# A gated projection by Strassen's scheme: seven block products for eight on one core of a Trainium2

## The chip, the cores and the metric

The kernel is one program on one NeuronCore of a Trainium2 chip. Its metric is the device time of one execution, in microseconds (us). Three runs took 3548.36, 3549.2 and 3543.41 us; the median is 3548.36.

## What is computed

Two transformer blocks of two layers each run one after the other on 512 tokens of width 1024, all in float32. The second block's feed-forward parts are gated, and there are two of them per layer (ffn1 and ffn2), around a mixer:

```python
D_MODEL, SEQ, DEPTH, D_FF = 1024, 512, 2, 2816

def swiglu(h, w_gu, w_down):
    gu = h @ w_gu                                   # (512, 1024) @ (1024, 2 * 2816)
    g, u = gu[..., :D_FF], gu[..., D_FF:]
    return (jax.nn.silu(g) * u) @ w_down

def second_block(x, ...):
    for l in range(DEPTH):
        x = x + 0.5 * swiglu(rmsnorm_2(x, ffn1_norm[l]), ffn1_w_gu[l], ffn1_w_down[l])
        x = x + hybrid_mixing(rmsnorm_2(x, mix_norm[l]), ...)
        x = x + 0.5 * swiglu(rmsnorm_2(x, ffn2_norm[l]), ffn2_w_gu[l], ffn2_w_down[l])
    return rmsnorm_2(x, final_norm)
```

## The kernel before, in words

Activations lie transposed: channel on the 128 partitions, token along the free axis, so x_lat is 8 tiles of 128 x 512. Every float32 product is made of three products in the fp32r format: each operand is split into a high part (a copy rounded to fp32r) and a low part (the operand less its high part), and TensorE adds low weight x high input, high weight x low input and high weight x high input (L803 to L805).

The program is a list of stages; each engine walks it with its own instruction queue, and semaphores order them. A linear stage goes by chunks, one chunk being 128 output channels. For chunk g the SP queue loads the weight into w_raw (two slots in turn, `load_chunk`), ScalarE makes the high part w_hi_sb (`split`, L1380), VectorE the low part w_lo_sb (`split`, L1769), and TensorE runs kt x 3 matmuls of 512 columns, kt being 8 for an input of 1024 channels and 11 for the input of a down projection. ScalarE starts the high part of chunk g once TensorE has finished chunk g - 2, which had the same slot.

The gated stages are of the kind `linear_glu`. There are two layers, two parts and two groups of FG = 11 tiles of 128 channels, so 8 such stages and 88 steps of i. A step is two chunks: the gate's into bank 0 and the up projection's into bank 1. VectorE multiplies the gate by rstd2, the inverse root of the mean square of the input (L2228), ScalarE takes silu (L1691), VectorE multiplies the up projection by rstd2 (L2231) and by silu (L2236), ScalarE makes the high part of the result (L1405) and VectorE its low part (L1835). These steps stand in a hardware loop (`Fori`). After each gated stage a `linear_r` stage multiplies the 11 middle tiles by the down projection and adds the result to x_lat (L2165).

The input of a gated stage is x scaled by the norm's gain, without rstd: in the final `linear_r` stage before it (`final=True`), each finished tile of x_lat is scaled by VectorE (L2182, `prep`), ScalarE makes its high and VectorE its low part, while GpSimd squares the tile and adds it to a running sum (`sum_squares`, L2322 to L2325). In the first group's stage TensorE turns the sum into the mean (`norm_sum`, L812), ScalarE takes the root and VectorE the reciprocal (L1774, `deferred_rstd`).

The lines that the rows below name beside these: L1801 is a multiply and add of VectorE for block 1's conditioning, L2257 finds the maximum of attention scores in PSUM, L2354 is GpSimd's scaling of attention weights, L1672 is a copy of a bank by ScalarE.

```python
for k in range(kt):
    nc.tensor.matmul(dst, wl, hi[:, k, 0:n], start=(k == 0), stop=False)
    nc.tensor.matmul(dst, wh, lo[:, k, 0:n], start=False, stop=False)
    mm = nc.tensor.matmul(dst, wh, hi[:, k, 0:n], start=False, stop=(k == kt - 1))
```

Of the kernel before, what the change touches and what calls it, by code (L numbers as in the profile page):

```python
# [101 lines left out]
def build_program(nc, a, out):  # L102
    from contextlib import ExitStack
    ctx = ExitStack()
    with ctx:
# [27 lines left out]
        m2h = place("m2h", [P, FG, T], F32R, mid0)  # L133
        m2l = place("m2l", [P, FG, T], F32R, mid0 + FG * T * 4)
# [8 lines left out]
        h2h = place("h2h", [P, KD, T], F32R, z0)  # L143
        h2l = place("h2l", [P, KD, T], F32R, z0 + KD * T * 4)
        w_raw = place("w_raw", [P, 2, WMAX])
        w_hi_sb = place("w_hi_sb", [P, 2, WMAX], F32R)
        w_lo_sb = place("w_lo_sb", [P, 2, WMAX], F32R)
# [39 lines left out]
        def x_square(n):  # L187
# [14 lines left out]
                 "fox_vt fox_vc fox_a fox_e fox_c c_hi c_lo c_rows sel_done o_zero r_const bd_zero pool_s pool_m pool_y pool_t pool_hi pool_lo "  # L202
                 "x_sq x_sum rows_zero rows_turned rows_copied silu_done x_turned x_copied y_ready y_turned y_copied y_scaled "
                 "dve_chain act_chain pool_chain").split()
        dma_names = ("w_loaded0 w_loaded1 mod_loaded0 mod_loaded1 mod_loaded2 mod_loaded3 fd_loaded0 fd_loaded1 fd_loaded2 "
                     "ctx_loaded konst_loaded rows_loaded "
                     "x_loaded rope_loaded ws_loaded rf_loaded mla_loaded bd_loaded stored").split()
# [3 lines left out]
        fd_loaded = [S[f"fd_loaded{i}"] for i in range(3)]  # L211

# [37 lines left out]

        Stage("setup", {})
        Stage("mod", {})
        for l in range(L):
# [31 lines left out]
            for g in range(FF1_GROUPS):  # L285
# [4 lines left out]
                Stage("linear_r", dict(r_taken=8, sumsq=1 * last, norm_t=8 * ends, h_hi=8 * ends, h_lo=8 * ends,  # L290
                                       sq_part=int(split_sq > 0), sq_last=split_sq), 8,
                      src="w_ff2", l=l, sets=more, gate=gate(1), group=g, final=last, kt=KD,
                      prep=(R_F1, hh_lat, hl_lat) if ends else None, block2=ends)
        lat = ("lat",)
        for l in range(L):
# [6 lines left out]
            for part in ("ffn1", "mix", "ffn2"):  # L302
                if part == "mix":
# [11 lines left out]
                    Stage("linear_r", dict(r_taken=8, sumsq=1, norm_t=8, h_hi=8, h_lo=8), 8, src="w_out_2", l=l, sets=lat,  # L315
                          gate=one, group=None, final=True, kt=KD, prep=(R_F2 + KD * l, h2h, h2l), block2=True)
                else:
                    for g in range(F2_GROUPS):
                        n1 = int(g == 0)
                        Stage("linear_glu", dict(gate_taken=FG, up_taken=FG, silu_ready=FG, t_ready=FG, mid_hi=FG, mid_lo=FG,  # L320
                                                 sum_ready=n1, root_ready=n1, rstd_ready=n1), 2 * FG, l=l, sets=lat,
# [20 lines left out]
        def next_kt(st):  # L342
            i = linear.index(st)
            return kt_of(linear[i + 1]) if i + 1 < len(linear) else None
# [185 lines left out]
        def late_square(st, s):  # L530

            return glu_up if st.block2 else sq_late[s]
# [1876 lines left out]
```

## Time and profile before

| | |
|---|---|
| median of three runs | 3548.36 us (3543.41 to 3549.2) |
| span of the profiled execution | 3545.8 us, 47285 instructions |
| TensorE (PE) busy | 3438.6 us, 97% |
| weight loads (PEld) busy | 2871.9 us, 81% |
| VectorE (DVE) busy | 1832.1 us, 52% |
| ScalarE (ACT) busy | 1226.1 us, 35% |
| GpSimd (POOL) busy | 362.9 us, 10% |
| mean of the DMA engines | 30% busy, 89 GB/s |

The page gives no time of the profiled execution beside its span; the span lies 2.6 us below the median of the runs. Busy time is the sum of durations, where overlapping ones count once. A matmul's duration is modelled and overlaps that of the next, so what it costs is read from the distance between starts.

### The profile page before, as it was taken

What the parts mean: (1) busy time and instruction counts of PE and PEld (TensorE: products, weight loads), DVE (VectorE), ACT (ScalarE), POOL (GpSimd) and SP (SyncE); (2) the same over time, 40 slices, a digit from 0 to 9 for tenths busy, and PEclk for the clock granted to TensorE, in tenths of its full rate; (3) what the DMA queues carried; (4) which work ended last, traced back from release to release, by engine and by line L of the source; (5) the groups of instructions that cost most, each with busy time, mean ns of one, the idle gap of its engine ahead of it and who ended that gap; (6) DMA issues with size and microseconds to landing.
All of it is one profiled execution on the core that took longest, in us unless ns stands there. A gap on an engine that the chain in (4) does not pass through costs nothing.

```text
span 3545.8 us, 47285 instructions
## 1 busy us (share of the span) xinstructions
PE 3438.6 (97%) x17172; PEld 2871.9 (81%) x17172; DVE 1832.1 (52%) x2781; ACT 1226.1 (35%) x1930; POOL 362.9 (10%) x403
## 2 busy tenths in 40 slices
PE   9989999999999999999999989999999999899999
PEld 5879888888878878888888677888888886778887
DVE  6755866554356444354345655434543455654343
ACT  4455222122146432233222364323232223643232
POOL 0012300000202200010001223000200011230001
PEclk9989999999999999999999999999999999999999
DMA  6300243334220123333333301333333333023332
GB/s 223 117 24 13 95 136 113 119 121 134 60 72 25 48 83 96 100 96 95 95 94 107 89 25 51 98 97 99 95 95 95 95 101 83 25 60 95 98 98 89
DMA packets 551252, 314.76 MB, mean 89 GB/s; under 512 B 31102, under 2 KB 524888, under 8 KB 551128
## 3 DMA queue, kind: packets, MB, share of 16 engines
q1 hardware_dynamic: 550608, 312.99, 29.7%
q8 instruction: 76, 1.25, 0.2%
q14 instruction: 48, 0.39, 0.0%
q10 hardware_dynamic: 520, 0.13, 0.0%
HBM read 310.98 MB, written 2.10 MB: 88 GB/s over the span
## 4 chain that ended last, share of the span: by engine, by line
PE 88%; DVE 5%; ACT 4%; issue 2%; POOL 1%; DMA 0%; SPq 0%; DVEq 0%; ACTq 0%; POOLq 0%
PE ps L803 26%; PE ps L805 25%; PE ps L804 25%; PE ps L1349 3%; PE ps L1325 1%; DVE nmax L2257 1%; PE ps L958 1%; DVE scr L1946 1%; PE ps L1291 1%; ACT scr L1720 1%; ACT z L1720 1%; PE ps L1292 1%; ACT w_hi_sb L1380 1%; DVE hl_ctx L1835 1%; DVE hl_lat L1934 0%
## 5 line engine op out<-in xcount | busy, mean ns | idle before, releaser
L1769 DVE TENSOR_TENSOR w_lo_sb<-w_raw,w_hi_sb 128x1024 fp32r<-128x1024 f32 (+1 forms) x460 | 588.6, 1280 | 1231.3 <-ACT w_hi_sb L1380 1228.9
L1380 ACT ACTIVATE w_hi_sb<-w_raw 128x1024 fp32r<-128x1024 f32 (+1 forms) x460 | 506.3, 1101 | 1375.6 <-PE ps L805 1347.4
L803 PE MATMUL ps<-hh_lat,w_lo_sb 128*128 128x512 f32 x1808 | 719.4, 398 | 6.3 <-DVE w_lo_sb L1769 1.9
L804 PE MATMUL ps<-hl_lat,w_hi_sb 128*128 128x512 f32 x1808 | 705.2, 390 | 0.0
L805 PE MATMUL ps<-hh_lat,w_hi_sb 128*128 128x512 f32 x1808 | 704.8, 390 | 0.0
L803 PEld LDWEIGHTS ps<-hh_lat,w_lo_sb 128*128 128x128 f32 x1808 | 340.5, 188 | 85.1 <-issue 6.8
L804 PEld LDWEIGHTS ps<-hl_lat,w_hi_sb 128*128 128x128 f32 x1808 | 340.6, 188 | 74.8 <-issue 6.3
L805 PEld LDWEIGHTS ps<-hh_lat,w_hi_sb 128*128 128x128 f32 x1808 | 340.1, 188 | 71.8
L803 PE MATMUL ps<-h2h,w_lo_sb 128*128 128x512 f32 x704 | 275.2, 391 | 1.9 <-DVE z L2228 1.5
L803 PE MATMUL ps<-m2h,w_lo_sb 128*128 128x512 f32 x704 | 273.9, 389 | 0.0
L804 PE MATMUL ps<-h2l,w_hi_sb 128*128 128x512 f32 x704 | 273.9, 389 | 0.0
L805 PE MATMUL ps<-h2h,w_hi_sb 128*128 128x512 f32 x704 | 273.9, 389 | 0.0
L805 PE MATMUL ps<-m2h,w_hi_sb 128*128 128x512 f32 x704 | 273.9, 389 | 0.0
L804 PE MATMUL ps<-m2l,w_hi_sb 128*128 128x512 f32 x704 | 273.9, 389 | 0.0
L803 PE MATMUL ps<-m1h_lat,w_lo_sb 128*128 128x512 f32 x512 | 200.4, 391 | 2.7 <-DVE x_ctx L2165 2.7
L804 PE MATMUL ps<-m1l_lat,w_hi_sb 128*128 128x512 f32 x512 | 199.5, 390 | 0.0
L805 PE MATMUL ps<-m1h_lat,w_hi_sb 128*128 128x512 f32 x512 | 199.3, 389 | 0.0
L2322 POOL TENSOR_TENSOR x_ctx<-x_lat 128x512 f32<-128x512 f32 x7 | 7.3, 1042 | 1578.1 <-DVE x_lat L2165 1578.1
L803 PEld LDWEIGHTS ps<-h2h,w_lo_sb 128*128 128x128 f32 x704 | 132.1, 188 | 31.1 <-DVE z L2228 2.3
L804 PEld LDWEIGHTS ps<-h2l,w_hi_sb 128*128 128x128 f32 x704 | 132.1, 188 | 27.8 <-issue 0.5
L805 PEld LDWEIGHTS ps<-h2h,w_hi_sb 128*128 128x128 f32 x704 | 132.1, 188 | 27.6
L2354 POOL TENSOR_SCALAR scr<-scr,rinv 128x768 f32<-128x768 f32 (+4 forms) x120 | 89.4, 746 | 635.4 <-DVE rinv L2268 634.9
(329 smaller groups left out, 5520.8 us busy)
## 6 DMA issues: line engine op xcount, KB each, us to landing
w_raw<-in_ffn_w_gu SPq DMA_DIRECT2D x176, 512.0 KB, 3.8
w_raw<-in_w_ff SPq DMA_DIRECT2D x128, 512.0 KB, 4.1
w_raw<-in_ffn_w_down SPq DMA_DIRECT2D x64, 704.0 KB, 4.5
z<-in_w_mod SPq DMA_DIRECT2D x64, 512.0 KB, 5.2
w_raw<-in_w_in SPq DMA_DIRECT2D x56, 512.0 KB, 3.9
w_raw<-in_w_out SPq DMA_DIRECT2D x32, 512.0 KB, 3.9
scr<-in_w_mod SPq DMA_DIRECT2D x16, 512.0 KB, 5.2
scr<-in_w_mod SPq DMA_DIRECT2D x2, 2048.0 KB, 14.6
```

Of the source, the lines that this page charges most:

```text
L803: nc.tensor.matmul(dst, wl, hi[:, k, 0:n], start=(k == 0), stop=False)
L804: nc.tensor.matmul(dst, wh, lo[:, k, 0:n], start=False, stop=False)
L805: mm = nc.tensor.matmul(dst, wh, hi[:, k, 0:n], start=False, stop=(k == kt - 1))
L958: mm = nc.tensor.matmul(bank(5 + n % 3)[0:2, :], silu_c[:, :, k], mod_slot(n)[:, k, :], start=(k == 0), stop=(k == KD - 1))
L1291: nc.tensor.matmul(dst[:, c0:c1], q, k_hi[:, hd // 4, c0:c1], start=True, stop=False)
L1292: mm = nc.tensor.matmul(dst[:, c0:c1], q, k_lo[hd // 4][:, c0:c1], start=False, stop=True)
L1325: mm = nc.tensor.transpose(bank(4 + i % 2)[:, j * P:(j + 1) * P], p[:, kt * P:(kt + 1) * P], ident)
L1349: mm = nc.tensor.matmul(bank(6 + hd % 2)[:, qt * P:(qt + 1) * P], val, att_pt(st, v, kt * P, (kt + 1) * P), start=(kt == 0), stop=(kt == n ...
L1380: nc.scalar.activation(w_hi_sb[:, slot, 0:width], w_raw[:, slot, 0:width], ACT.Copy).then_inc(S["w_hi"], 1)
L1720: nc.scalar.activation(att_p(st, u, n), s_slot(st, u, n), ACT.Exp, bias=nmax[:, i:i + 1], scale=q_scale(st, u) if st.first else 1.0, accum ...
L1769: nc.vector.tensor_tensor(w_lo_sb[:, slot, 0:width], w_raw[:, slot, 0:width], w_hi_sb[:, slot, 0:width].bitcast(F32), ALU.subtract).then_i ...
L2354: nc.gpsimd.tensor_scalar(pr, pr, rinv[:, i:i + 1], 0.0, ALU.mult, ALU.add).then_inc(S["p_norm"], 1)
```

## The change

It concerns the `linear_glu` stages and what makes their input. The eight products of 128-channel blocks in a step (gate and up, two halves of the 1024 input channels, two halves of the 512 tokens) become seven products of sums of blocks, in the form with shared sums. A product has 4 tiles of input channels and 256 tokens.

Inputs: in the final `linear_r` stage before, `prepare7` makes seven operand sets h7 from x (X11, X12 - X11 and so on), with ScalarE's scaled copy and high parts and VectorE's sums and low parts; group 1 uses the same sets again.

Weights: SP loads a pair (gate and up block, 1 MB in two issues) into one of two slots; GpSimd makes three sums s1, s2, s4 and a21 - a11 in place (`pair_sums`); ScalarE and VectorE make high and low parts of the seven weight operands (`product_hi`, `product_lo`, 512 wide), in a ring of seven slots and four products ahead of TensorE.

Products: TensorE runs them in the order m1, m4 of the step before, m5, m2, m6, m3, m7. Some are added onto others in their bank; others are joined by ScalarE's copies (e1, e5, e2) and VectorE's sums into gate and up. GpSimd multiplies silu by rstd2. The steps are written out, and no longer in a hardware loop.

```diff
 TensorE, linear_glu
-                        run_linear(st, free, up_banks, {"lat": st.x}, inputs="h_lo" if first else None, sums=first)
+                        def product(m, i, before=None):
+                            n = ORDER[m, i]
+                            pe.wait_ge(S["pr_lo"], st.at("pr_lo", n + 1))
+                            adds = m in ("m6", "m3", "m7", "m4")
+                            w, dst, x_lo = home.slots[SLOT[m]], product_bank(m, i), x7_lo(m)
+                            for k in range(QK):
...
+                                nc.tensor.matmul(dst, wl, x_hi, start=(k == 0 and m in ("m1", "m5", "m2")), stop=False,
+                                                 skip_group_check=adds)
+                                nc.tensor.matmul(dst, wh, x_lo[:, k, :], start=False, stop=False, skip_group_check=adds)
+                                mm = nc.tensor.matmul(dst, wh, x_hi, start=False, stop=(k == QK - 1), skip_group_check=adds)
+                            mm.then_inc(S["pr_done"], 1)
+                        for i in range(FG):
...
+                            if i >= 2:
+                                pe.wait_ge(S["t_ready"], st.at("t_ready", i - 1))
+                            product("m1", i)
+                            if i:
+                                pe.wait_ge(S["c_out"], st.at("c_out", 3 * i))
+                                product("m4", i - 1)
+                                pe.wait_ge(S["c_out"], st.at("c_out", 3 * i - 1))
+                            product("m5", i)
...
+                            pe.wait_ge(S["m_out"], st.at("m_out", 3 * i + 1))
+                            product("m6", i)
+                            pe.wait_ge(S["m_out"], st.at("m_out", 3 * i + 2))
+                            product("m3", i)
+                            pe.wait_ge(S["m_out"], st.at("m_out", 3 * i + 3))
+                            product("m7", i)
 ScalarE
+                def product_hi(glu, n):
...
+                    nc.scalar.activation(glu.home.slots[SLOT[m]][:, 0, :], product_source(glu, m, i), ACT.Copy
+                                         ).then_inc(S["pr_hi"], 1)
+                        def take(dst, m, i):
...
+                            nc.scalar.activation(dst[:, :], product_bank("m6" if m == "u2" else m, i), ACT.Copy
+                                                 ).then_inc(S["m_out"], 1)
 VectorE, linear_glu
+                def product_lo(glu, n):
...
+                    nc.vector.tensor_tensor(w[:, 1, :], product_source(glu, m, i), w[:, 0, :].bitcast(F32), ALU.subtract
+                                            ).then_inc(S["pr_lo"], 1)
+                        for i in range(FG):
+                            n = ORDER["m1", i] + AHEAD
+                            if i:
+                                up_second(i - 1)
+                            product_lo(st, n)
+                            product_lo(st, n + 1)
+                            if i:
+                                product_lo(st, n + 2)
+                                n += 1
+                                gated(i - 1)
+                            product_lo(st, n + 2)
+                            if i:
+                                mid_low(i - 1)
+                            gate_first(i)
+                            product_lo(st, n + 3)
+                            product_lo(st, n + 4)
+                            gate_second(i)
+                            product_lo(st, n + 5)
 GpSimd
+                def pair_sums(st, i):
...
+                    nc.gpsimd.tensor_tensor(s1, a21, a22, ALU.add).then_inc(S["pr_sum"], 1)
...
+                    nc.gpsimd.tensor_tensor(s2, s1, a11, ALU.subtract).then_inc(S["pr_sum"], 1)
...
+                    nc.gpsimd.tensor_tensor(s4, a12, s2, ALU.subtract).then_inc(S["pr_sum"], 1)
+                    nc.gpsimd.tensor_tensor(a21, a21, a11, ALU.subtract).then_inc(S["pr_sum"], 1)
...
+                        for i in range(FG):
+                            if i + 1 < FG:
+                                pair_sums(st, i + 1)
...
+                            nc.gpsimd.tensor_tensor(st.home.sr[:, :], st.home.silu[:, :], rstd2, ALU.mult
+                                                    ).then_inc(S["sr_ready"], 1)
```

Of VectorE's helpers, `up_second`, `gate_first` and `gate_second` add a product in PSUM (256 columns) to what ScalarE copied; `gate_second` also multiplies the gate by rstd2 (512) and, in a first group's first step, makes the reciprocal; `gated` multiplies the up projection by sr, one half from SBUF (256) and one from PSUM (256); `mid_low` makes the low part of the middle (512). The pair of step i is loaded once the low part of m4 of step i - 2 is made.

## Rows read from the trace of the kernel before

**Rows 1.** The page: busy time (part 1) and TensorE's granted clock in 40 slices (part 2).

```profile
PE 3438.6 (97%) x17172; PEld 2871.9 (81%) x17172; DVE 1832.1 (52%) x2781; ACT 1226.1 (35%) x1930; POOL 362.9 (10%) x403
...
PEclk9989999999999999999999999999999999999999
```

**Rows 2.** Table of windows, ten steps of a gated stage: window, length, busy us of each engine.

```profile
1784.05:1893.50 109.45, 109.45 (x484) 90.65 (x483) 50.79 (x61) 34.19 (x40) 0.00 (x0) 1.00 0.34 99
```

**Rows 3.** Timeline of TensorE in the same kind of stage, first and last of 54: start, us.

```profile
2499.78 0.39 PE L804 MATMUL ps<-h2l,w_hi_sb 128*128 128x512 f32 x1
...
2511.80 0.39 PE L803 MATMUL ps<-m2h,w_lo_sb 128*128 128x512 f32 x1
```

**Rows 4.** Timeline of TensorE in block 1, first and last of 48 matmuls of 256 columns.

```profile
500.03 0.28 PE L803 MATMUL ps<-m1h_ctx,w_lo_sb 128*128 128x256 f32 x1
...
505.66 0.28 PE L805 MATMUL ps<-m1h_ctx,w_hi_sb 128*128 128x256 f32 x1
```

**Rows 5.** VectorE: timeline of a gated stage, then groups by form (busy us, mean ns).

```profile
2455.37 1.23 DVE L1769 TENSOR_TENSOR w_lo_sb<-w_raw,w_hi_sb 128x1024 fp32r<-128x1024 f32 x1 [1.27 <-ACT w_hi_sb L1380]
2456.52 0.68 DVE L2228 TENSOR_TENSOR z<-ps,x_ctx 128x512 f32<-128x512 f32 x1
...
L2236 DVE TENSOR_TENSOR z<-z 128x512 f32<-128x512 f32 x88 | 60.9, 693 | 10.1
...
L2204 DVE TENSOR_TENSOR z<-z 128x256 f32<-128x256 f32 x32 | 13.4, 418 | 0.0
```

**Rows 6.** Timeline of VectorE in a linear_r stage of block 1, operations issued back to back.

```profile
349.48 0.48 DVE L2165 SCALAR_TENSOR_TENSOR x_ctx<-ps,modv,x_ctx 128x256 f32<-128x256 f32 x1
349.87 0.74 DVE L1801 SCALAR_TENSOR_TENSOR z<-z,silu_c 128x512 f32<-128x512 f32 x1
```

**Rows 7.** ScalarE's groups by form.

```profile
L1405 ACT ACTIVATE m2h<-z 128x512 f32 x80 | 50.6, 632 | 224.0 <-DVE z L2236 224.0
...
L1672 ACT ACTIVATE z<-ps 128x256 f32<-128x256 f32 x32 | 12.0, 376 | 0.0
```

**Rows 8.** Timeline of GpSimd in block 1, two operations in a row.

```profile
1208.94 1.04 POOL L2324 TENSOR_TENSOR z<-x_lat 128x512 f32<-128x512 f32 x1 [3.12 <-DVE x_lat L2165]
1210.06 1.28 POOL L2325 TENSOR_TENSOR z<-z 128x512 f32<-128x512 f32 x1
```

**Rows 9.** Timelines of GpSimd and VectorE in narrow windows of block 1, by start.

```profile
358.71 1.06 POOL L2324 TENSOR_TENSOR z<-x_lat 128x512 f32<-128x512 f32 x1 [6.18 <-DVE x_ctx L2165]
358.79 1.53 DVE L1801 SCALAR_TENSOR_TENSOR z<-z,silu_c 128x512 f32<-128x512 f32 x1
359.85 1.62 POOL L2325 TENSOR_TENSOR z<-z 128x512 f32<-128x512 f32 x1
360.25 1.78 DVE L1801 SCALAR_TENSOR_TENSOR z<-z,silu_c 128x512 f32<-128x512 f32 x1
```

**Rows 10.** Timelines of VectorE and GpSimd at the end of block 1.

```profile
1598.03 0.75 DVE L1835 TENSOR_TENSOR hl_lat<-x_ctx,hh_lat 128x512 fp32r<-128x512 f32 x1 [0.70 <-ACT hh_lat L1405]
1598.31 1.61 POOL L2325 TENSOR_TENSOR x_ctx<-x_ctx,z 128x512 f32<-128x512 f32 x1
```

**Rows 11.** Timelines of GpSimd and VectorE in block 1's attention.

```profile
305.41 0.91 POOL L2354 TENSOR_SCALAR scr<-scr,rinv 128x768 f32<-128x768 f32 x1 [4.51 <-DVE rinv L2268]
305.55 0.95 DVE L2257 TENSOR_REDUCE nmax<-ps 128x1 f32<-128x768 f32 x1
```

**Rows 12.** VectorE's reciprocals of rstd2, group by form.

```profile
L1774 DVE RECIPROCAL x_ctx<-x_ctx 128x512 f32<-128x512 f32 x6 | 20.1, 3353 | 18.5 <-ACT x_ctx L1388 18.5
```

**Rows 13.** DMA issues: KB each, median us to landing.

```profile
w_raw<-in_ffn_w_gu SPq DMA_DIRECT2D x176, 512.0 KB, 3.8
w_raw<-in_ffn_w_down SPq DMA_DIRECT2D x64, 704.0 KB, 4.5
```

**Rows 14.** Table of windows, two stretches of attention; PEclk is the third number from the end.

```profile
2081.80:2160.00 78.20, 66.16 (x514) 61.90 (x514) 41.47 (x111) 60.66 (x169) 31.23 (x55) 1.00 0.01 2
197.70:218.20 20.50, 15.48 (x60) 12.85 (x60) 10.88 (x33) 8.38 (x23) 2.90 (x6) 0.50 0.00 0
```

More of the change, by code:

```diff
@@ L1654, in _ @@
                             gained(KD - 2)
+                        elif st.spec.get("prep7") is not None:
+                            for c in range(0, st.chunks, 2):
+                                pair(c, st.kt)
                         else:
@@ L1695, in _, with done @@
-                        use_table(ACT.Silu)
-                        with act.Fori(0, FG - 1) as i:
-                            pair(i, KD)
-                        pair(FG - 1, next_kt(st))
+                        home = st.home
+                        nxt = stages[stages.index(st) + 1]
+                        use_table(ACT.Sqrt if st.group == 0 else ACT.Silu)
+                        def done(m, i):
+                            act.wait_ge(S["pr_done"], st.at("pr_done", ORDER[m, i] + 1))
@@ L2168, in pair @@
                                 o.then_inc(S["r_taken"], 1)
+                                if glu and late and s == 1:
+                                    product_lo(glu, 3)
+                                if st.spec.get("prep7") is not None:
+                                    prepare7(c + s)
                                 if ends:
@@ L2189, in _ @@
                             due.extend(zip(feed_ends[id(st)], (2, 6)))
+                        elif st.spec.get("prep7") is not None:
+                            for c in range(0, st.chunks, 2):
+                                pair(c, st.kt)
                         else:
@@ new lines, in gate_second @@
+                        def gate_second(i):
+                            done("m3", i)
+                            dve.wait_ge(S["m_out"], st.at("m_out", 3 * i + 3))
+                            nc.vector.tensor_tensor(home.gate[:, second], product_bank("m3", i), home.e2[:, :], ALU.add
+                                                    ).then_inc(S["c_out"], 1)
+                            if i == 0 and st.group == 0:
+                                deferred_rstd(st)
+                            dve.wait_ge(S["c_out"], st.at("c_out", 3 * i + 2))
+                            nc.vector.tensor_tensor(home.gate[:, :], home.gate[:, :], rstd2, ALU.mult).then_inc(S["gate_taken"], 1)
```

426 lines of the change are left out of this document (333 added, 93 removed).

## The prediction

> **What bounds the kernel now.** I began with the page: TensorE is busy for 97% of the span, with its clock at nine tenths or more of full speed nearly everywhere [rows 1]. A high share alone does not say that TensorE is the limit, so next I read a stretch inside one gated stage, by the table of windows [rows 2]: ten of the stage's eleven steps of i, from one read of the gate's bank to the tenth after it, take 109.45 us, or 10.94 us per i, with TensorE busy throughout, VectorE busy for 50.79, ScalarE for 34.19 and GpSimd for nothing. So the gated stages are bound by TensorE. GpSimd is free there, and VectorE is free for half of the time. The change spends both.
>
> A matmul's duration in the trace overlaps its neighbour's, so what an instruction costs is the distance from start to start. At 512 columns 53 distances take 12.02 us, 0.2268 each [rows 3]; 48 of them are 10.89 us, which is the step of i but for 0.05. At 256 columns 47 distances take 5.63 us, 0.1198 each [rows 4], though every matmul there has its own weight load, as it would have in the change.
>
> **TensorE's part.** It removes 48 matmuls of 512 columns per i and adds 7 x 4 x 3 = 84 of 256. In columns that is one eighth less. In time it is 84 x 0.1198 = 10.06 us against 10.89, only 0.83 less, because half the columns cost 53% of the time. There are 4 blocks of gated work (two layers, two parts) of 2 groups of 11: 88 steps. If TensorE stays the limit, this is -73 us, and that is all there is to win. The Trainium skill ("TensorE: Matmul & The Clock Gate", Back-to-back issue gap) gives N/2.4 + 2.5 ns, thus 109 ns at 256 columns and 216 at 512; by that estimate the removed and added matmuls would differ by 1.2 us per i, or -105 us. This case's trace shows 120 ns [rows 4], and the measured distance is used.
>
> **VectorE's part, per i.** Removed: two low parts of 1024 and four operations of 512, 5.2 us in all. Added: seven low parts of 512; the gate's product with rstd2 (512); the low part of the middle (512); half a product of 256 from SBUF; and four operations of 256 that read one operand from PSUM. The distance of a 1024 low part to what follows is 1.15 us for a duration of 1.23 [rows 5], so 0.08 is hidden by the pipeline; a 512 operation lasts 0.69 [rows 5] and so takes about 0.62. The 256 one lasts 0.42 [rows 5], about 0.35 of distance, and a 256 operation that reads PSUM takes 0.39 from start to start [rows 6]. Sum: 9 x 0.62 + 0.35 + 4 x 0.39 = 7.5 us. It would fit beside 10.06 if nothing held VectorE up.
>
> **ScalarE's part, per i.** Seven high parts of 512, silu and the middle's high part at 0.63, three bank reads of 256 at 0.38 [rows 7]: 9 x 0.63 + 3 x 0.38 = 6.8 us. It fits, and nothing is charged for it.
>
> **GpSimd's part, per i, and the term that decides.** Nothing ran there. Now there are four sums or differences of block pairs (512, both operands in SBUF) and one product silu x rstd2. Alone a GpSimd sum of 512 lasts 1.28 us, and a product 1.04 [rows 8]. Both engines then read two SBUF operands at once, and the trace shows what happens. GpSimd's product runs from 358.71 to 359.77 [rows 9]; VectorE's operation, issued at 358.79, ends at 360.32, 0.55 us after GpSimd is through, although its like takes 0.74. GpSimd's sum, issued at 359.85, ends at 361.47, and VectorE's next at 362.03, again 0.55 later. They take turns, whole instruction by whole instruction: between GpSimd's ends at 359.77 and 361.47 lie 1.70 us, which hold one VectorE operation (0.55) and one sum (1.15). The form that the change uses, TENSOR_TENSOR, behaves alike [rows 10]: GpSimd's sum issued at 1598.31 lasts 1.61 instead of 1.28, because VectorE's ends only at 1598.78; GpSimd's end comes 1.14 after that. A VectorE operation that reads PSUM is not held: 0.95 beside a GpSimd operation that runs from 305.41 to 306.32 [rows 11]. But that one has no SBUF operand at all, and the four in the change have one beside the bank. If those are held too, nothing is covered and the step is the ceiling below. The Trainium skill ("SBUF — State Buffer", Who interferes with whom) draws the line at two SBUF inputs, which would leave the four free; no row here shows that form.
>
> GpSimd holds the port for 4 x 1.15 + 0.91 = 5.5 us per i (0.91 is the product's 1.04 less the 0.13 that separates 1.28 from 1.15). **Ceiling:** VectorE always has something queued, so each of these holds stands before it: 7.5 + 5.5 = 13.0 us per i. **Floor:** the port alone, perfectly packed: four pairs of 1.70, one of 0.55 + 0.91, four left-over operations at 0.62, the 256 one at 0.35: 11.1 us. Even the floor is above 10.94. Between them counts how much of GpSimd's time falls beside the four PSUM reads (1.56 us). GpSimd is busy for some 45% of the step, thus 0.7 is covered: **12.3 us per i**. VectorE, not TensorE, sets the step, and 88 x (12.3 - 10.94) = **+120 us**.
>
> What queues behind a held VectorE: at the head of each i it reads product m7 out of the bank that m4 of the i before is to be added to, and TensorE's m4 waits for that read. Low part m6, whose place in the ring lies only four products ahead, stands behind the same read. So a delay of VectorE reaches TensorE within two products, 2.9 us.
>
> **The edges.** In a stage's start the first four low parts are made in the stage before (4 x 0.62 = 2.5 us off the first step); at its end m4 of the last i waits for VectorE's read, with nothing else to multiply, and the next stage's first low part of 1408 follows: about 2.5 us on. I take these as equal. In the four stages with group 0 three things are new. The 3.35 us reciprocal [rows 12] falls on the engine that now sets the pace. In the stage before, making seven operand sets costs VectorE, by the same rates, about 3.1 us per chunk, beside 1.15 + 0.66 and 2.1 of GpSimd's squares: 7.0 against a chunk of 24 x 0.2268 = 5.44, in two chunks: 3.1. And m6 needs the sets made last, behind two more copies and subtractions: about 3. Together 9.5 x 4 = **+38 us**. Bounds: 0 if all of it stays covered, 80 if the chunks before are held too.
>
> **The loads** keep their 1 MB per i, now as two issues at once behind one wait. One lands after 3.8 us and 704 KB after 4.5 [rows 13], so 512 KB more is some 1.9 us more: 5.7 in all, hidden by a step of 12. The issue queue has nothing behind it but the next pair. No charge.
>
> **Sum:** the profiled span 3545.8 + 120 + 38 = 3704; the median of the runs, 3548.4, is 2.6 above that span, so 3706 us. A difference of 0.2%, 7 us, is about what a measurement of this kernel can tell from none.
>
> **Rivals.** (A) *TensorE stays the limit.* Then -73, and edges of about 8 x 1 for the bubble at a stage's end and 4 x 4 for its start: 3548 - 49 = 3499 us. For it: by duration alone VectorE's 7.5 and GpSimd's 5.5 both fit in 10.06. Against it: the two take turns, and their sum counts [rows 9, 10]. It holds only if VectorE's 7.5 us and what it is kept waiting stay under 10.06, that is if less than half of GpSimd's 5.5 stands before it; by rows the port's holds alone (9 x 0.55 + 0.29 + 5.5) sum to 10.7 without a single gap. Chance 0.13. (B) *Near the floor:* GpSimd hides well, 11.1 per i: +14 + 38, 3600 us. A part of the forecast's case, its lower end. (C) *The pair's load is late:* GpSimd's first sum waits for it, and everything of the next i behind that. If two loads need 8 us and not 5.7, the step grows by about 1: 3795 us. Chance 0.04. (D) *It comes out even,* with half of the holds hidden and small edges: 3548. Chance 0.03. The clock could add to the slow side: TensorE would idle for 18% of a step. There is full clock over 78 us with TensorE busy for 85% of them, and half clock in a stretch at 76% [rows 14]; so I charge nothing and leave room above.
>
> **Numbers.** The exclusive port, from floor to ceiling, has 0.80. Range 3560 to 3800: below it the floor with no edges (3562), above it 13.0 per i (+181) with edges of 70. The chances follow: slower 0.84 (0.80 + 0.04), same 0.03, faster 0.13.
>
> **What would show it.** The distance between two reads of product m2's bank near 12.3 us (10.1 would make A right); TensorE near 10.06 us of issue per i with waits named as VectorE's reads of ps or its low parts; VectorE's 512 operations with a mean far over 0.69 (some 1.2) and a maximum near 1.8; GpSimd's sums above 1.28; 256-column matmuls still 0.120 apart. Low parts at 0.69 beside a busy GpSimd would overturn the central step.

## The result and the profile after

The changed kernel takes 3744.14 us (median of 4 runs, 3742.58 to 3744.99) against 3548.11 for the kernel before (4 runs, 3543.41 to 3549.2): a ratio of 1.0553, 95% interval 1.0538 to 1.0567. It is 5.5% slower, or 196 us. Forecast were 3706 us, in a range of 3560 to 3800.

The page of the kernel after, parts 1 and 2, as [rows 1]:

```profile
PE 3449.5 (92%) x20340; PEld 3025.5 (81%) x20340; DVE 2443.7 (65%) x3549; ACT 1481.8 (40%) x2682; POOL 1027.7 (27%) x843
...
PEclk9989999999999999989999998999899999989999
```

Over the whole span no engine looks like the limit: TensorE has fallen from 97% to 92%, VectorE has 65%. One has to go into the stage. The table of windows, from the first read of product m2's bank to the eleventh, in a group 1 and in the group 0 before it (columns as in [rows 2], so length, then busy us of TensorE, its weight loads, VectorE, ScalarE and GpSimd, then granted clock):

```profile
1816.05:1938.60 122.55, 104.11 (x824) 102.08 (x823) 116.27 (x142) 57.35 (x118) 72.73 (x49) 0.97 0.31 84
1618.03:1742.36 124.33, 108.58 (x837) 106.55 (x837) 118.94 (x143) 59.60 (x121) 70.03 (x47) 0.95 0.30 83
```

Ten steps last 122.55 us where they lasted 109.45 [rows 2], and now VectorE is busy for 95% of them. The waits of TensorE's weight loads say for what (us in total, times, longest):

```profile
PEld ps L1321 <- DVE f_up L2527: 151.7, 87, 3.6
PEld ps L1321 <- DVE marks L2412: 34.8, 8, 6.5
```

The first row is once in each of the 88 steps but one: m4 waits for VectorE's read of m7's bank. The second is only in the starts of the group-0 stages: 8 waits of up to 6.5 us for the operand sets of the last tiles. Why VectorE is late stands in its groups by form, and in GpSimd's (busy us, mean ns, idle before):

```profile
L2010 DVE TENSOR_TENSOR f_slot<-pair_raw,f_slot 128x512 fp32r<-128x512 f32 x352 | 366.1, 1041 | 91.1 <-ACT f_slot L1543 90.9
L2010 DVE TENSOR_TENSOR f_slot<-f_sums,f_slot 128x512 fp32r<-128x512 f32 x264 | 308.1, 1191 | 8.0 <-ACT f_slot L1543 7.7
...
L2076 DVE TENSOR_TENSOR f_m_lo<-f_t,f_m_hi 128x512 fp32r<-128x512 f32 x88 | 130.4, 1482 | 5.6 <-ACT f_m_hi L1569 5.6
```

```profile
L2680 POOL TENSOR_TENSOR pair_raw<-pair_raw 128x512 f32<-128x512 f32 x88 | 151.0, 1716 | 0.0
L2675 POOL TENSOR_TENSOR f_sums<-f_sums,pair_raw 128x512 f32<-128x512 f32 x88 | 137.6, 1564 | 6.9
```

An operation of VectorE on 512 columns lasts 0.69 us alone [rows 5]; here the mean of a low part is 1.04 to 1.19, and the middle's low part, which nearly always meets GpSimd, has 1.48. GpSimd's sums have 1.56 and 1.72 against 1.28 alone [rows 8]. The alternation itself, at the turn of a step (VectorE's timeline, then GpSimd's, start and duration):

```profile
1864.18 1.00 DVE L2010 TENSOR_TENSOR f_slot<-pair_raw,f_slot 128x512 fp32r<-128x512 f32 x1 [1.88 <-ACT f_slot L1543]
1865.11 1.78 DVE L2076 TENSOR_TENSOR f_m_lo<-f_t,f_m_hi 128x512 fp32r<-128x512 f32 x1
1866.81 0.41 DVE L2511 TENSOR_TENSOR f_gate<-ps,f_e 128x256 f32<-128x256 f32 x1
```

```profile
1863.35 1.29 POOL L2675 TENSOR_TENSOR f_sums<-f_sums,pair_raw 128x512 f32<-128x512 f32 x1
1864.72 1.62 POOL L2679 TENSOR_TENSOR f_sums<-pair_raw,f_sums 128x512 f32<-128x512 f32 x1
1866.30 1.75 POOL L2680 TENSOR_TENSOR pair_raw<-pair_raw 128x512 f32<-128x512 f32 x1
```

GpSimd's sum from 1864.72 ends at 1866.34; VectorE's low part, begun inside it, ends 0.55 later, at 1866.89. This is the picture of [rows 9]. The next operation of VectorE, which reads one operand from PSUM and one from SBUF, takes 0.41 us beside the sum that runs from 1866.30: it is not held. No row of before showed that form. Over all 88 it has a maximum of 0.42.

The starts of group 0 were the other place. TensorE's timeline, the matmuls that it waited for (the time in brackets), at the first of the four:

```profile
1603.76 0.39 PE L1321 MATMUL ps<-h_hi,f_slot 128*128 128x256 f32 x1 [2.15 <-DVE marks L2412]
1610.71 0.58 PE L1321 MATMUL ps<-h_hi,f_slot 128*128 128x256 f32 x1 [6.34 <-DVE marks L2412]
1615.26 0.58 PE L1321 MATMUL ps<-h_hi,f_slot 128*128 128x256 f32 x1 [1.83 <-DVE h_lo_t L2076]
```

and VectorE's in the same stretch:

```profile
1594.35 1.75 DVE L2010 TENSOR_TENSOR f_slot<-pair_raw,f_slot 128x512 fp32r<-128x512 f32 x1
1596.30 1.50 DVE L2010 TENSOR_TENSOR f_slot<-f_sums,f_slot 128x512 fp32r<-128x512 f32 x1 [0.20 <-ACT f_slot L1543]
1597.73 1.76 DVE L2010 TENSOR_TENSOR f_slot<-pair_raw,f_slot 128x512 fp32r<-128x512 f32 x1
1599.41 0.74 DVE L2437 SCALAR_TENSOR_TENSOR x_lat<-ps,modv,x_lat 128x512 f32<-128x512 f32 x1
...
1606.34 0.74 DVE L2437 SCALAR_TENSOR_TENSOR x_lat<-ps,modv,x_lat 128x512 f32<-128x512 f32 x1
...
1621.62 3.34 DVE L2015 RECIPROCAL x_ctx<-x_ctx 128x512 f32<-128x512 f32 x1
```

TensorE had nothing left of the old stage from about 1594, but VectorE updated x for tile 7, of which the operand sets are made, only at 1606.34. Ahead of tile 6's update stand three low parts of the next stage, each held by GpSimd's sums for that same stage.

By TensorE's first and last product, a group-1 stage of gated work lasts 136.4 us (135.4 to 137.2) where it lasted 119.7, and a group-0 stage 152.7 (151.2 to 154.1) where it lasted 122.6: 4 x 16.7 + 4 x 30.1 = 187 us. Of the 195 us between the two profiled spans some 7 more lie ahead of the first product, where TensorE stands still for 2.0 us in three of the four group-0 stages. The group-1 part is nearly all in the steps.

### The profile page after: what moved, and what is told of

Same layout as the page of the kernel before. It is cut to its first block, busy times and chain, and to the rows that moved or that the text cites. A ratio compares the mean times of both kernels' runs of the same rounds, so it can differ in the third digit from the quotient of the medians.

```text
span 3740.8 us, 54435 instructions
## 1 busy us (share of the span) xinstructions
PE 3449.5 (92%) x20340; PEld 3025.5 (81%) x20340; DVE 2443.7 (65%) x3549; ACT 1481.8 (40%) x2682; POOL 1027.7 (27%) x843
## 4 chain that ended last, share of the span: by engine, by line
PE 62%; DVE 22%; issue 6%; ACT 5%; DMA 3%; POOL 1%; SPq 0%; ACTq 0%; DVEq 0%; POOLq 0%
PE ps L909 15%; PE ps L910 15%; PE ps L911 15%; DVE f_slot L2010 9%; DVE f_m_lo L2076 2%; PE ps L1496 2%; PE ps L1321 2%; DMA pair_raw<-in_ffn_w_gu 2%; PE ps L1324 2%; PE ps L1323 2%; PE ps L1472 1%; DVE f_t L2535 1%; ACT f_slot L1543 1%; DVE nmax L2581 1%; DVE f_up L2527 1%
## 5 line engine op out<-in xcount | busy, mean ns | idle before, releaser
L1321 PE MATMUL ps<-h_hi,f_slot 128*128 128x256 f32 x2464 | 735.1, 298 | 186.6 <-DVE f_up L2527 134.1
L1324 PE MATMUL ps<-h_hi,f_slot 128*128 128x256 f32 x2464 | 721.7, 293 | 0.0
L1321 PEld LDWEIGHTS ps<-h_hi,f_slot 128*128 128x128 f32 x2464 | 498.7, 202 | 214.4 <-DVE f_up L2527 151.7
L1324 PEld LDWEIGHTS ps<-h_hi,f_slot 128*128 128x128 f32 x2464 | 498.6, 202 | 0.0
L909 PE MATMUL ps<-hh_lat,w 128*128 128x512 f32 x1104 | 444.5, 403 | 4.0 <-DVE w L2000 1.9
L910 PE MATMUL ps<-hl_lat,w 128*128 128x512 f32 x1104 | 431.4, 391 | 0.0
L911 PE MATMUL ps<-hh_lat,w 128*128 128x512 f32 x1104 | 430.9, 390 | 0.0
L2010 DVE TENSOR_TENSOR f_slot<-pair_raw,f_slot 128x512 fp32r<-128x512 f32 x352 | 366.1, 1041 | 91.1 <-ACT f_slot L1543 90.9
L1323 PE MATMUL ps<-h_lo_x,f_slot 128*128 128x256 f32 x1408 | 412.9, 293 | 0.0
L2010 DVE TENSOR_TENSOR f_slot<-f_sums,f_slot 128x512 fp32r<-128x512 f32 x264 | 308.1, 1191 | 8.0 <-ACT f_slot L1543 7.7
L1323 PE MATMUL ps<-h_lo_t,f_slot 128*128 128x256 f32 x1056 | 309.3, 293 | 0.0
L909 PE MATMUL ps<-f_m_hi,f_w 128*128 128x512 f32 x704 | 274.9, 391 | 0.0
L911 PE MATMUL ps<-f_m_hi,f_w 128*128 128x512 f32 x704 | 274.0, 389 | 0.0
L909 PEld LDWEIGHTS ps<-hh_lat,w 128*128 128x128 f32 x1104 | 208.3, 189 | 54.3 <-issue 6.3
L911 PEld LDWEIGHTS ps<-hh_lat,w 128*128 128x128 f32 x1104 | 207.9, 188 | 44.3
```

Source lines behind the costliest of these rows:

```text
L1321: nc.tensor.matmul(dst, wl, x_hi, start=(k == 0 and m in ("m1", "m5", "m2")), stop=False, skip_group_check=adds)
L1323: nc.tensor.matmul(dst, wh, x_lo[:, k, :], start=False, stop=False, skip_group_check=adds)
L1324: mm = nc.tensor.matmul(dst, wh, x_hi, start=False, stop=(k == QK - 1), skip_group_check=adds)
L2010: nc.vector.tensor_tensor(w[:, 1, :], product_source(glu, m, i), w[:, 0, :].bitcast(F32), ALU.subtract).then_inc(S["pr_lo"], 1)
```

## The experiments

The theory: VectorE and GpSimd exclude each other while both read two SBUF operands, so their times add up in a step, and VectorE's delay reaches TensorE through the read of m7's bank. The rivals: VectorE's own work, ScalarE's copies or the pair's load set the step; and for what the forecast missed, the reciprocal, the order of VectorE's queue, or GpSimd's work at a start. In the table a step is a tenth of the window between the first and the eleventh read of m2's bank, averaged over the four stages of a group. For the kernel before, the read is that of the gate's bank; in its group 0 the first of them comes late, behind the reciprocal, which makes that window shorter. Some expectations count from silu to silu, which gives the kernel after 12.06, because it leaves out the longer way into the first step. Each ratio is to runs of the kernel before made beside the variant, whose medians lie between 3547.4 and 3552.8. The variants e1, e4, e6, e7 and e8 have two runs each, e10 and e11 six, the others four.

| kernel | time, us | ratio to before, 95% interval | step, group 1 | step, group 0 |
|---|---|---|---|---|
| before | 3548.11 | 1 | 10.94 | 10.74 |
| after | 3744.14 | 1.0553 [1.0538, 1.0567] | 12.27 | 12.42 |
| e1_pool_writes | 3571.93 | 1.0068 [1.0048, 1.0088] | 9.97 | 10.77 |
| e8_double_sum | 3809.75 | 1.0738 [1.0717, 1.0759] | 13.13 | 13.20 |
| e4_sr_dve | 3728.29 | 1.0509 [1.0486, 1.0532] | 12.09 | 12.22 |
| e2_sums_dve | 3686.78 | 1.0392 [1.0375, 1.0410] | 11.43 | 11.90 |
| e3_all_dve | 3681.96 | 1.0381 [1.0364, 1.0398] | 11.39 | 11.85 |
| e5_order | 3597.26 | 1.0138 [1.0121, 1.0154] | 10.21 | 10.78 |
| e6_start_writes | 3718.08 | 1.0480 [1.0459, 1.0501] | | |
| e7_copy_recip | 3729.27 | 1.0511 [1.0489, 1.0532] | | |
| e9_start_order | 3573.24 | 1.0068 [1.0050, 1.0086] | 10.20 | 10.70 |
| e10_up_first | 3573.32 | 1.0073 [1.0058, 1.0087] | 10.22 | 10.59 |
| e11_early_x | 3572.25 | 1.0068 [1.0053, 1.0083] | 10.22 | 10.71 |

**e1_pool_writes: GpSimd writes, but reads nothing.** Each of its five operations of a step becomes eight writes of a constant to the same tile, with the same waits and signals. The sums and the product themselves are left out, so what the kernel computes is not the block.

```diff
+                def pool_op(dst, real, i=1):
+                    if not i:
+                        return real()
+                    for k in range(8):
+                        o = nc.gpsimd.memset(dst[:, 64 * k:64 * k + 64], 0.0)
+                    return o
...
-                    nc.gpsimd.tensor_tensor(s1, a21, a22, ALU.add).then_inc(S["pr_sum"], 1)
+                    pool_op(s1, lambda: nc.gpsimd.tensor_tensor(s1, a21, a22, ALU.add), i).then_inc(S["pr_sum"], 1)
```

> In the steps of the gated stages each of GpSimd's five operations is replaced by eight memsets of 64 columns onto the same tile: GpSimd is busy about as long (0.1 to 0.15 us each, some 1 us per operation) but reads nothing from SBUF. The pair sums (after the first step) and silu x rstd2 are left out. Theory (exclusive port): VectorE's 512 operations fall from a mean of 1.0 to 1.5 us back to 0.69, the step from 12.05 to TensorE's 10.1 to 10.3 us, and the kernel to about 3744 - 88 x 1.85 = 3580 us. Rival (the results of GpSimd's chain of sums come late, whatever the port): GpSimd takes as long as before, so the step stays near 12 and VectorE's operations wait for semaphores instead; total near 3740.

Window of the same ten steps, and VectorE's low parts by form:

```profile
1801.34:1901.06 99.72, 99.19 (x824) 98.98 (x825) 74.35 (x142) 58.68 (x119) 36.10 (x388) 1.00 0.37 104
```

```profile
L2010 DVE TENSOR_TENSOR f_slot<-pair_raw,f_slot 128x512 fp32r<-128x512 f32 x352 | 256.6, 729 | 123.9 <-ACT f_slot L1543 123.1
L2010 DVE TENSOR_TENSOR f_slot<-f_sums,f_slot 128x512 fp32r<-128x512 f32 x264 | 187.7, 713 | 135.9 <-ACT f_slot L1543 135.3
```

With GpSimd still busy for 3.6 us a step but not reading, the low parts are back at 0.71 to 0.73, VectorE's busy time falls from 116.27 to 74.35, TensorE is busy throughout and the step is 9.97. So it was neither VectorE's own work, nor ScalarE, nor the load: none of them changed, and none shows. That leaves what GpSimd does. Its writes keep it busy for only half as long as its sums did (36.10 against 72.73 us), so by the step alone its chain of sums could also have been late; but a low part that has begun and lasts 1.04 to 1.19 us instead of 0.72 waits for no result, and VectorE was busy for 95% of the window. What holds it is the reading of operands. But the kernel is still 24 us over the kernel before, though in group 1 each step now saves 0.97. That loss lies in the starts of group 0: these stages last 133 us here, 20 more than the group-1 stages (113), where the kernel before has 3 more.

**e8_double_sum: one hold more.** The first sum of each pair is made twice.

```diff
+                    if i:
+                        link(nc.gpsimd.tensor_tensor(s1, a21, a22, ALU.add))
                     nc.gpsimd.tensor_tensor(s1, a21, a22, ALU.add).then_inc(S["pr_sum"], 1)
```

> The change with one more GpSimd operation per step: the pair's first sum is made twice, the second after the first. Theory (each GpSimd operation that reads SBUF is paid by VectorE with its hold of 1.15 us, less what falls beside reads of PSUM): 0.8 to 1.15 us more per step, in 80 steps, total 3744 + 64 to 92 = 3808 to 3836 us; VectorE's low parts get longer again. Rival (GpSimd's hold is absorbed by slack in the queues): under 0.3 us per step, under 3770 us.

```profile
1825.10:1956.11 131.01, 107.20 (x824) 104.96 (x823) 125.87 (x141) 58.20 (x118) 89.81 (x59) 0.95 0.28 79
```

The step grows by 0.86 us, and VectorE's busy time by 0.96 a step, though nothing was added to VectorE. The forecast's price of a hold was 1.15, of which some falls beside reads of PSUM or waits.

**e4, e2 and e3: the work moved to VectorE,** where it cannot collide. In e4_sr_dve VectorE makes silu x rstd2, in e2_sums_dve the four sums of pairs 1 to 10, in e3_all_dve both.

```diff
+                        def silu_rstd(i):
...
+                            nc.vector.tensor_tensor(home.sr[:, :], home.silu[:, :], rstd2, ALU.mult).then_inc(S["sr_ready"], 1)
...
+                            nc.vector.tensor_tensor(dst, x, y, op).then_inc(S["pr_sum"], 1)
...
+                                silu_rstd(i - 1)
...
+                            pair_sum(i + 1, 0)
...
+                            pair_sum(i + 1, 1)
```

> Only silu x rstd2 is moved to VectorE; the four sums stay on GpSimd. Theory: VectorE gains 0.62 of its own and loses one hold of 0.9: step 11.6 to 12.0, total 3715 to 3740 us. Rival (GpSimd's place in the loop matters most: the product silu x rstd2 stands between silu and the sums of the next pair): step near 11, total 3650.

> The four sums of each pair after a stage's first are moved from GpSimd to VectorE; GpSimd keeps silu x rstd2. Theory (exclusive port): VectorE's own work is 7.5 + 4 x 0.62 = 10.0 us per step, and GpSimd's 0.9 is partly in its way: step 10.3 to 10.9, total about 3744 - 88 x 1.5 = 3615 us (3590 to 3650). Rival (VectorE is simply short of time, so work moved onto it lengthens the step by what it lasts, 4 x 0.62 = 2.5): step 14.5, total 3960.

> All five of GpSimd's operations of a step are on VectorE, GpSimd does nothing in a step. Theory: VectorE 7.5 + 5 x 0.62 = 10.6 us per step, no wait for the port: step 10.6 to 10.8, total 3590 to 3620 us; VectorE's 512 operations at 0.69. It should come within 0.3 us per step of the variant with only the sums moved. Rival (VectorE simply short of time): step above 15.

All three are faster than the kernel after, the four sums by 57 us, the product by 16, both by 62. That more work on the engine that sets the pace makes the kernel faster is the plainest evidence for the port. The time of e4 is as expected. But e2 and e3 both miss: forecast were steps of 10.3 to 10.9 and of 10.6 to 10.8, and they take 11.43 and 11.39. VectorE's timeline shows what is left:

```profile
1817.83 0.41 DVE L2542 TENSOR_TENSOR f_t<-ps,f_sr 128x256 f32<-128x256 f32 x1
1819.34 0.69 DVE L2010 TENSOR_TENSOR f_slot<-pair_raw,f_slot 128x512 fp32r<-128x512 f32 x1 [1.09 <-ACT f_slot L1543]
```

No operation is held, and yet VectorE stands still for 1.09 us in each step, for a high part that ScalarE makes behind its read of m5's bank; that read waits for TensorE's m5, which stands behind m4, which waits for VectorE's read of m7's bank. A loop of waits among three engines, each busy for less than the step (100.27, 101.51 and 56.93 us in the 112.78 of ten steps).

**e5_order: the loop opened.** Beyond e3, ScalarE makes the next m1's high part before it reads m5's bank, and VectorE reads m7's bank at the end of its own step, ahead of a low part.

```diff
-                            take(home.e5, "m5", i)
                             product_hi(st, n + 2)
+                            take(home.e5, "m5", i)
...
-                            if i:
-                                up_second(i - 1)
...
                             gate_second(i)
                             pair_sum(i + 1, 3)
+                            up_second(i)
                             product_lo(st, n + 5)
```

> As the variant with all five operations on VectorE, with two places in the queues moved: ScalarE makes the high part of the next m1 before it reads the bank of m5, and VectorE reads m7's bank before the low part of the next m2, not behind it. Measured without the move: 11.4 us per step, with VectorE idle some 0.8 us of it. Theory (the rest is a loop of waits: TensorE's m4 waits for VectorE's read of m7, ScalarE's read of m5 waits for TensorE, VectorE's low part waits for ScalarE): the step falls to VectorE's own 10.6 to 10.8 us, total near 3682 - 88 x 0.7 = 3620 us. Rival (VectorE's own work was underestimated and lasts 11.4): no change, 3680 us.

VectorE's timeline at the same place, and the window of ten steps:

```profile
1811.19 0.42 DVE L2542 TENSOR_TENSOR f_t<-ps,f_sr 128x256 f32<-128x256 f32 x1
1811.52 0.69 DVE L2010 TENSOR_TENSOR f_slot<-pair_raw,f_slot 128x512 fp32r<-128x512 f32 x1
```

```profile
1803.71:1905.88 102.17, 99.99 (x821) 98.76 (x821) 100.95 (x190) 59.83 (x118) 0.00 (x0) 1.00 0.36 101
```

The idle time is gone, the step is 10.21 and the kernel 85 us faster than e3, more than expected: VectorE's own work is 10.1 a step, not 10.6. The two moves were made together, so what each is worth is not known. VectorE (100.95 of 102.17) and TensorE (99.99) are now both full. In group 1 the steps save 0.73 each against before; the time is still 49 us over before, so all of that and more is lost at the edges of the stages, most of it at the starts of group 0: group-0 stages of 132.3 to 136.5 us beside group-1 stages of 115.9 to 117.8.

**e6_start_writes: what GpSimd costs at a start.** In the kernel after, and only in the stage before group 0, the first pair's sums and the squares are writes of a constant.

```diff
+                            if st.spec.get("prep7") is not None:
+                                if m:
+                                    link(pool_op(sq_tmp2, None))
+                                o = pool_op(sq_sum2, None, v=80000.0)
```

> The change as it is, but around the start of a gated part GpSimd only writes: the first pair's sums and the squares of the stage before (the sum of squares is left out, and a constant stands for it) are memsets of about the same length. Steps are untouched. Theory (the port also delays VectorE while it makes the seven operand sets and the first low parts): VectorE saves 6 to 9 us before each first group's stage, and those stages' TensorE time falls from 151 to 154 to some 145 us; total 3744 - 4 x 7 - 4 x 2 = 3710 us. Rival (there the serial chain of ScalarE's copies and VectorE's sums decides, not the port): under 2 us per start, 3735 us or more.

The time falls by 26 us, 6.5 per start, between what the theory and the rival had, nearer the theory. In the profiled executions the group-0 stages are shorter by 4.9 in the mean and the group-1 stages by 0.9, and TensorE stands still for 0.3 us instead of 2.0 ahead of the first product. The two medians rest on two and four runs.

**e7_copy_recip: without the reciprocal.** It is left out in the gated stages.

```diff
+                    if st.kind == "linear_glu":
+                        nc.vector.memset(rstd2, 0.1).then_inc(S["rstd_ready"], 1)
```

> The change with the reciprocal of the root left out in the gated stages (a memset of the tile stands for it). Theory (VectorE sets the pace there, so its 3.35 us count in full): 4 x 2.9 = 12 us less, 3732 us, and the gap of TensorE of some 3 us in the first step is gone. Rival (it is hidden, as it nearly was before the change): 3744 us.

The time falls by 15 us, 3.7 for each of the four: its duration of 3.34 as in [rows 12], and little more.

**e9_start_order: VectorE's order at a start.** Beyond e5, VectorE makes the first pair's sums too, and updates x for tiles 6 and 7 before it turns to the next stage's low parts. ScalarE's high parts for these products are put in the matching order.

```diff
+                                early = glu and st.final and late
+                                if early:
+                                    pass
+                                elif glu and late:
                                     for n in range(3 * (s == 0)):
                                         product_lo(glu, n)
...
+                                if early and s == 0:
+                                    product_lo(glu, 0)
+                                    prepare7(c + s, [lambda: first_sum(0)])
+                                elif early:
+                                    product_lo(glu, 1)
+                                    prepare7(c + s, [lambda: product_lo(glu, 2), lambda: first_sum(1)])
```

> The kernel of e5_order, with the start of the second gated stage's groups in another order as well: in the stage that prepares the tiles (prep7), the sums of the first pair are made on VectorE (they were GpSimd's), and VectorE's update of x for tiles 6 and 7 no longer stands behind the first low parts; the low parts and sums fill the time in which VectorE would wait for ScalarE's high parts. Everything is computed. Theory (what e5_order has left over the kernel before is the group-0 starts, set by VectorE's order between the last updates of x and the first products): the update of tile 7 comes some 5 us earlier, each of the four group-0 stages is 5 to 6 us shorter than e5_order's 132.3 to 136.5, and the time is about 3575 us (3570 to 3580). Rival (the start is set by the chain of ScalarE's squares and high parts and GpSimd's multiplications, and VectorE's order there only moves a wait): under 2 us per start, 3590 us or more.

3573.24 us: 24 less than e5, 6 per start, as the theory had it. Counted from the update of tile 5, that of tile 7 comes after 13.7 us, where e5 and the kernel after have 18.7, and the group-0 stages last 128.3 to 131.5.

**e10_up_first and e11_early_x: further down the same road, without effect.** What e9 leaves is this (VectorE's timeline in the first step):

```profile
1614.92 3.34 DVE L2026 RECIPROCAL x_ctx<-x_ctx 128x512 f32<-128x512 f32 x1
1618.29 0.69 DVE L2559 TENSOR_TENSOR f_gate<-f_gate,x_ctx 128x512 f32<-128x512 f32 x1
1618.90 0.69 DVE L2597 TENSOR_TENSOR pair_raw<-pair_raw 128x512 f32<-128x512 f32 x1
1619.50 0.42 DVE L2564 TENSOR_TENSOR f_up<-ps,f_e 128x256 f32<-128x256 f32 x1
```

TensorE's m4 waits for the last of these. So e10 puts that read ahead of the reciprocal, and e11 moves the updates of tiles 6 and 7 into gaps further ahead.

```diff
                             if i == 0 and st.group == 0:
+                                up_second(i)
+                                product_lo(st, ORDER["m1", i] + AHEAD + 5)
                                 deferred_rstd(st)
```

```diff
+                                    last = glu and st.final and c + s == KD - 3
+                                    prepare7(c + s, [lambda: update(c + 2, 0)] if last else ())
```

> The kernel of e9_start_order, and in the first step of each group-0 stage VectorE reads m7's bank and makes the low part of the next m2 before the reciprocal of the root of the mean square (3.34 us) and the product of the gate with it; they stood behind it. Everything is computed. In e9_start_order's trace TensorE stands 4.78 us between the next m1 and m4, whose bank VectorE reads only at 1619.50 us, behind the reciprocal. Theory (that wait is TensorE's own and only part of it comes back as a wait for ScalarE's read of m1's bank, which stands behind the silu and so behind the reciprocal): some 3 us less per group-0 stage, 4 x 3 = 12 us in all, about 3561 us (3558 to 3566). Rival (VectorE is behind anyway, by its backlog, and the wait only moves to m6 of the second step): under 1 us per stage, 3569 us or more.

> The kernel of e10_up_first, and in the stage that prepares the tiles VectorE's update of x for tile 6 stands before the last low part of tile 5 and that for tile 7 before the last low part of tile 6, where VectorE waited for ScalarE's high parts; ScalarE prepares tile 6 before the high part of m1. Everything is computed. In e9_start_order TensorE had finished chunk 6 at 1590.2 us + 2.7 us of the next chunk, and VectorE reads it at 1592.97; from there to the last low part (1607.2) VectorE has hardly a gap. Theory (the group-0 start is set by VectorE's queue, so each microsecond of its idle time that is filled before 1593 us brings the first products forward by one): 1.5 to 2.4 us per group-0 stage beyond e10_up_first, 6 to 10 us in all, about 3553 us if e10_up_first gives 3561. Rival (the last tile's chain through ScalarE and GpSimd's squares, which hold the port beside it, sets the end): under 0.5 us per stage, within 2 us of e10_up_first.

Both rivals won: 3573.32 and 3572.25 us, no different from e9, though with runs of one kernel 13 us apart a few us could not be told. The same view of e10:

```profile
1619.04 0.41 DVE L2566 TENSOR_TENSOR f_up<-ps,f_e 128x256 f32<-128x256 f32 x1
1619.37 0.68 DVE L2021 TENSOR_TENSOR f_slot<-pair_raw,f_slot 128x512 fp32r<-128x512 f32 x1
1619.96 3.35 DVE L2026 RECIPROCAL x_ctx<-x_ctx 128x512 f32<-128x512 f32 x1
...
1625.52 0.69 DVE L2021 TENSOR_TENSOR f_slot<-f_sums,f_slot 128x512 fp32r<-128x512 f32 x1 [0.28 <-ACT f_slot L1543]
```

The edit does what it says: the read stands before the reciprocal. But TensorE's matmuls then wait for low parts, which are now behind it. Over the whole kernel their waits for f_up fell from 29.8 to 19.0 us, those for low parts rose from 29.0 to 34.9 and those for ScalarE's copies from 5.2 to 10.1: the sum stays. In the profiled executions the group-0 stages are 1.0 us shorter than in e9, of the 3 that were expected. At a start VectorE's queue is full, so this order chose mostly which product waits. In e11 the updates that come earlier also bring GpSimd's squares earlier, and the holds only move: the last low part of tile 5 lasts 1.75 us where e9 had 0.96, the first low part of tile 6 0.68 where e9 had 1.76. Its group-0 stages are 2.4 us shorter than e10's from first to last product, but TensorE's gap ahead of the first product has grown from 1.6 to 4.7 us in three of the four.

## Why the prediction was right, and where its sizes were off

**TensorE's part** held: e1, with TensorE alone as the limit, has a step of 9.97 us against 10.06.

**The port, the term that decides,** held in kind and in size. Forecast were 12.3 us between two reads of m2's bank; measured are 12.27 in group 1, inside floor and ceiling (11.1, 13.0). The parts came out a little otherwise. VectorE's own busy time is 7.4 a step (e1), as forecast (7.5); what GpSimd adds to it is (116.27 - 74.35)/10 = 4.2, not 4.8; and VectorE stands still for 0.6 a step, in six waits for ScalarE's high parts over the ten steps, which the forecast had at nothing, since it took VectorE to have something queued always. Two errors of 0.6 cancel: that the step agrees within 0.03 is luck, that it lies between floor and ceiling is not. That the PSUM reads go free is now seen; the line that the Trainium skill draws ("SBUF — State Buffer", Who interferes with whom), at two SBUF inputs, agrees with their 0.41 us.

Rival A (the durations fit beside one another, 3499) fell with the 12.27. B's floor is not reached. C, the late load: it lands after 5.1 us in the median, near the estimate of 5.7, and TensorE's waits name VectorE. D fell too.

**The reading of "what queues behind"** was right in its place: 151.7 us of waits for f_up. It was worth more than it was given: the order around that read and ScalarE's read of m5's bank cost 85 us together, as e5 against e3 shows, where no port collides. A VectorE step of 10.1 us needs no 11.4; only the loop through ScalarE and TensorE made it so. The forecast treated VectorE as a queue that is always full, and such a loop as a consequence of the port. The kernel after with only the order changed was not run; there VectorE stands still for 0.6 a step, so by an estimate from that at most 88 x 0.6 = 53 us of the 196 could come back.

**The edges are the step that failed in size.** Forecast: +38 us, 9.5 per group-0 start, nothing for group 1. Measured: a group-1 stage has +16.7, of which 11 steps of 1.33 make 14.6, so 2.1 are edge; a group-0 stage has +30.1 and 1.8 in the mean ahead of its first product, 17.3 beyond 11 such steps. That is 4 x 17.3 + 4 x 2.1 = 78 us, 40 more than forecast; less the 3 by which the steps came out shorter (88 x 1.33 = 117, not 120), that is the 37 between the span of 3704 that was forecast and the profiled 3741. Of the 17.3: the reciprocal is 3.7 (e7; forecast 3.35). GpSimd's squares and first sums cost 6.5 (e6, with what they cost in the chunks before and the steps behind). The forecast had charged the prepared chunks 3.1, the squares in it, and had not seen that four sums come on top: three of them each hold one of the low parts that stand before tile 6's update (1.75, 1.50, 1.76 us instead of 0.69). Tile 7's chain behind them had been given about 3; the wait of 6.34 for it is what e9's order shortens. The shares overlap, so they do not add up exactly, and up to 3.7 may be the clock's.

**The clock** was charged nothing. TensorE's clock stood at half for 259 us of the span, against 95 before, and steps with a half-clock stretch in them last 12.35 us on average, those without 11.92 (from silu to silu, 26 and 54 of them): 26 x 0.43 = 11 us at most, if the clock is the cause and not the sign of a longer wait. At the starts, from the first product to the first silu, 159 matmuls of 256 columns fell into stretches at half clock, where they lie 0.213 us apart instead of 0.120: 15 us in all, 3.7 per start, if none of it were hidden behind VectorE. No run separated the clock from the waits.

## What to carry to other kernels

An idle engine is not free work if it shares a port with the one that feeds the bottleneck: look in the trace for two of their operations side by side, and add their holds instead of laying them beside each other. Here even VectorE doing all of it was better (3682 against 3744), and the order around two reads of banks was worth more still (3597). Nor is a full queue the only way to lose the time of an engine: a ring of waits through three engines took 11.4 us a step where none had more than 10.2 of work. A saving of an eighth in columns was 7.6% in time by the measured distances (10.06 against 10.89), and eight stage edges are enough to eat it: the best version of this scheme, with everything computed, is 0.7% slower than the kernel before.

## What was not expected of the hardware

TensorE's clock at a start of group 0 (table of windows of the kernel after; granted clock is the third number from the end):

```profile
1604.30:1621.40 17.10, 8.92 (x35) 7.28 (x35) 14.10 (x17) 9.98 (x19) 8.97 (x6) 0.50 0.02 5
1584.00:1604.30 20.30, 16.01 (x77) 13.32 (x75) 16.51 (x20) 7.14 (x10) 11.58 (x8) 0.92 0.38 104
```

After TensorE had stood waiting more than once the clock went to the lower of its two levels, 1.2 GHz, and stayed there for 17.1 us, with TensorE still waiting for half of that. The same length of 17.1 us is in each of the four starts. What the lower level costs shows in the distances of TensorE's matmuls there, 0.21 us where [rows 4] has 0.12:

```profile
1616.71 0.41 PE L1321 MATMUL ps<-h_hi,f_slot 128*128 128x256 f32 x1
1616.93 0.41 PE L1323 MATMUL ps<-h_lo_t,f_slot 128*128 128x256 f32 x1
1617.14 0.41 PE L1324 MATMUL ps<-h_hi,f_slot 128*128 128x256 f32 x1
```

Inside the steps shorter stretches of 3.4 us come and go. [Rows 14] had shown full clock with TensorE busy for 85% of a stretch; here, over ten steps at 85% (104.11 of 122.55), the mean is 0.97.

GpSimd's writes of a constant do not hold VectorE: 388 of them in ten steps of e1, and VectorE's low parts at 0.71 to 0.73 us.
